# Expert weights fetched as two halves of feature rows, and asked for ahead of the down weights

## The reference

```python
for e in range(N_EXPERTS):            # 32 experts, D_EXPERT = 256
    y = (jax.nn.silu(t @ e_gate[e]) * (t @ e_up[e])) @ e_down[e]
    out = out + combine[:, e:e + 1] * y
```

## Time and profile before

| what | before |
|---|---|
| median of 3 runs | 840.44 us (839.94 to 841.41) |
| the profiled execution | 836.75 us, its span 834.9 us |
| PE busy | 757.1 us (91%) |
| DVE, ACT, POOL busy | 505.1, 428.7, 317.4 us |
| DMA | 160.41 MB, mean 192 GB/s |
| gate, up, down requests | 32 each, 1024.0 KB, median 18.0, 23.0 and 18.7 us to landing |
| chain that ended last | PE 63%, DMA 18%, DVE 7%, ACT 6% of the span |

### The profile page before, as it was taken

The page is one execution under the profiler, slowest core; times in us unless marked ns, Lnnn a source line. Parts: engine busy times, 40 slices in busy tenths (PEclk is TensorE's granted clock), DMA queues, the critical chain, the costliest instruction groups (busy, mean ns, idle before and its releaser), DMA issues.

```text
span 834.9 us, 10616 instructions
## 1 busy us (share of the span) xinstructions
PE 757.1 (91%) x3974; PEld 547.2 (66%) x3974; DVE 505.1 (60%) x774; ACT 428.7 (51%) x636; POOL 317.4 (38%) x240
## 2 busy tenths in 40 slices
PE   3899999999996888899899979999999999989983
PEld 3788888876664555478788856666666666656641
DVE  5641000007766888451347868888888877778827
ACT  6311102116555888630121448878877777677714
POOL 2513354615645776151001134444433333332212
PEclk9999999999999999999999999999999999999998
DMA  8371111100010000241671958999999999999379
GB/s 288 80 201 51 50 29 50 50 1 1 1 47 6 0 1 1 61 141 51 227 258 71 350 163 321 375 382 364 375 376 370 372 373 365 362 363 361 115 265 366
DMA packets 54949, 160.41 MB, mean 192 GB/s; under 512 B 9344, under 2 KB 24160, under 8 KB 46576
## 3 DMA queue, kind: packets, MB, share of 16 engines
q1 hardware_dynamic: 48352, 142.26, 47.3%
q0 software_dynamic: 6400, 16.92, 6.1%
q10 hardware_dynamic: 144, 0.52, 0.2%
HBM read 145.01 MB, written 18.87 MB: 196 GB/s over the span
## 4 chain that ended last, share of the span: by engine, by line
PE 63%; DMA 18%; DVE 7%; ACT 6%; issue 3%; SPq 2%; POOL 0%; DVEq 0%; POOLq 0%; ACTq 0%
DMA wgu<-in_expert_w_up 12%; PE ps L644 6%; PE ps L646 6%; PE ps L645 6%; PE ps L884 5%; PE ps L889 5%; PE ps L892 4%; PE ps L767 3%; PE ps L769 3%; PE ps L768 3%; PE ps L709 3%; PE ps L684 2%; PE ps L911 2%; PE ps L915 2%; PE ps L919 2%
## 5 line engine op out<-in xcount | busy, mean ns | idle before, releaser
L1632 DVE TENSOR_TENSOR wgulo<-wgu,unit 128x2048 fp32r<-128x2048 f32 x64 | 146.4, 2289 | 47.1 <-ACT unit L1174 46.8
L1174 ACT CAST unit<-wgu 128x2048 fp32r<-128x2048 f32 x64 | 122.0, 1907 | 49.2 <-DMA wgu<-in_expert_w_up 47.4
L1880 POOL DMA_INDIRECT expert_rows<-ysb,idx x32 | 53.9, 1685 | 152.2 <-ACT ysb L1221 143.6
L644 PE MATMUL ps<-hThi,whi 128*128 128x512 f32 x224 | 88.8, 396 | 4.2 <-DVE hTlo L1288 4.2
L1873 POOL DMA_INDIRECT xg<-h_rows,idx x32 | 69.3, 2164 | 57.2 <-PE ps L860 40.4
L646 PE MATMUL ps<-hThi,wlo 128*128 128x512 f32 x224 | 88.2, 394 | 0.0
L645 PE MATMUL ps<-hTlo,whi 128*128 128x512 f32 x224 | 88.1, 393 | 0.0
L884 PE MATMUL ps<-unit,xThi 128*80 128x512 f32 x256 | 72.4, 405 | 0.8 <-ACT xThi L1198 0.8
L1638 DVE TENSOR_TENSOR wdlo<-wd,unit 128x2048 fp32r<-128x2048 f32 x32 | 73.1, 2284 | 0.0
L889 PE MATMUL ps<-unit,xTlo 128*80 128x512 f32 x256 | 70.2, 396 | 0.0
L892 PE MATMUL ps<-wgulo,xThi 128*80 128x512 f32 x256 | 69.1, 391 | 0.0
(11 more groups left out here) (203 smaller groups left out, 1498.8 us busy)
## 6 DMA issues: line engine op xcount, KB each, us to landing
wgu<-in_expert_w_gate SPq DMA_DIRECT2D x32, 1024.0 KB, 18.0
wgu<-in_expert_w_up SPq DMA_DIRECT2D x32, 1024.0 KB, 23.0
wd<-in_expert_w_down SPq DMA_DIRECT2D x32, 1024.0 KB, 18.7
y<-expert_rows SPq DMA_DIRECT2D x16, 512.0 KB, 11.1
wraw<-in_w_in SPq DMA_DIRECT2D x14, 512.0 KB, 4.1
xin<-in_x SPq DMA_DIRECT2D x8, 512.0 KB, 5.5
xres<-in_x SPq DMA_DIRECT2D x16, 256.0 KB, 2.9
out<-fo SPq DMA_DIRECT2D x8, 512.0 KB, 7.6
```

Of the source, the lines that this page charges most:

```text
L644: nc.tensor.matmul(bank, whi[i % 2][:, k, :], hThi[:, k, cols], start=(k == 0), stop=False)
L1174: nc.scalar.copy(weight_unit(e, a)[:], raw_half(wgu, e, a)).then_inc(ahi_done, 1)
L1632: nc.vector.tensor_tensor(raw_half(wgulo, e, a), raw_half(wgu, e, a), weight_unit(e, a)[:].bitcast(F32), ALU.subtract).then_inc(alo_done, 1)
```

## The change

Gate and up of an expert are asked for in halves that match TensorE's halves: four requests of 512 KB (4 KB in one piece of each partition) in place of two of 1 MiB, each half behind its own `half_done` count, with a landing semaphore for each half, for which ScalarE waits before each half's cast. In the loop from expert 4 on, the two halves of expert e go ahead of the down weights of e-1. The down weights of expert 3 wait until the first two gathers have landed.

```diff
-        wgu_in = [sem(f"wgu_in{i}") for i in range(RING)]
+        wgu_in = [[sem(f"wgu_in{i}_{a}") for a in range(2)] for i in range(RING)]
...
-            def fetch_expert(e):
+            def fetch_half(e, h):
+                u = e % RING
+                a, b, c = load_expert(e, u, False)
+                ks = slice(4 * h, 4 * h + 4)
+                if e >= RING:
+                    sp.wait_ge(half_done, 2 * (e - RING) + 1 + h)
+                sp.dma_start(wgu[u][:, 0, ks], a[:, ks]).then_inc(wgu_in[u][h], 16)
+                sp.dma_start(wgu[u][:, 1, ks], b[:, ks]).then_inc(wgu_in[u][h], 16)
+
+            def fetch_down(e):
                 u = e % RING
                 a, b, c = load_expert(e, u, False)
                 if e >= RING:
-                    sp.wait_ge(half_done, 2 * (e - RING) + 2)
-                sp.dma_start(wgu[u][:, 0], a).then_inc(wgu_in[u], 16)
-                sp.dma_start(wgu[u][:, 1], b).then_inc(wgu_in[u], 16)
-                if e >= RING:
                     sp.wait_ge(down_done, e - RING + 1)
                 sp.dma_start(wd[u][:], c).then_inc(wd_in[u], 16)
+
+            def fetch_expert(e):
+                fetch_half(e, 0)
+                fetch_half(e, 1)
+                fetch_down(e)
...
             sp.wait_ge(out_mm, 2 * TT)
-            for e in range(2, N_EXP):
-                fetch_expert(e)
+            fetch_expert(2)
+            fetch_half(3, 0)
+            fetch_half(3, 1)
+            sp.wait_ge(xg_in[0], 16)
+            sp.wait_ge(xg_in[1], 16)
+            fetch_down(3)
+            for e in range(RING, N_EXP):
+                fetch_half(e, 0)
+                fetch_half(e, 1)
+                if e > RING:
+                    fetch_down(e - 1)
+            fetch_down(N_EXP - 1)
...
             def half_high(e, a):
 
                 u = 3 * e + a
-                if a == 0:
-                    act.wait_ge(wgu_in[e % RING], 32 * (e // RING + 1))
+                act.wait_ge(wgu_in[e % RING][a], 32 * (e // RING + 1))
```

More of the change, by code:

```diff
@@ L264, in encoder @@
         sq_done = sem("sq_done")
-        eps_added = sem("eps_added")
+        small_done = sem("small_done")
         rstd_a = sem("rstd_a")
@@ L356, in encoder @@
         y_put = [sem(f"y_put{i}") for i in range(2)]
-        v_hots = sem("v_hots")
         v_list_mm = sem("v_list_mm")
@@ L592, in _ @@
             with sp.If(n_ovf > 0):
-                sp.wait_ge(v_lists, 1)
+                sp.wait_ge(v_lists, 2)
                 with sp.Fori(0, N_OVF) as j:
@@ L954, in _ @@
             with pe.If(n_ovf > 0):
-                pe.wait_ge(v_hots, 1)
+                pe.wait_ge(v_lists, 1)
                 for c in range(2 * TT):
@@ L1221, in rows_out @@
                 nc.scalar.copy(ysb[e % 2][:].rearrange("q (n d) -> q n d", n=2), ps[0:CAP, b0:b0 + 2, :]).then_inc(y_out, 1)
-            nc.scalar.activation(junk[:], stat[:, 3, :], ACT.Silu).then_inc(junk_done, 1)
+            nc.scalar.activation(junk[:], stat[:, 3, :], ACT.Silu)
             half_high(0, 1)
@@ L1532, in experts_of @@
                                      misc[:, 12:12 + N_EXP].unsqueeze(1).to_broadcast([P, 2 * TG, N_EXP]), ALU.mult))
-                v.tensor_reduce(ek[:, 2 * TG * g:2 * TG * (g + 1)], mine, AX_X, ALU.add).then_inc(ek_done, 1)
+                v.tensor_reduce(ek[:, 2 * TG * g:2 * TG * (g + 1)], mine, AX_X, ALU.add)
             nc.vector.memset(hx[:], 0.0).then_inc(hx_zero, 1)
@@ L1624, in overflow_lists @@
                 steps_apart(*[v.tensor_tensor(ovf_tile[:, :, a, :], ovf_eq[:], wide(dvals[:, a, :], N_OVF), ALU.mult) for a in range(2)])
-                v.tensor_tensor(ovf_row[:], rows80.to_broadcast([P, 2 * TT, CAP]), wide(row, CAP), ALU.is_equal).then_inc(v_hots, 1)
+                v.tensor_tensor(ovf_row[:], rows80.to_broadcast([P, 2 * TT, CAP]), wide(row, CAP), ALU.is_equal).then_inc(v_lists, 1)
                 dve.wait_ge(v_list_mm, 1)
@@ L1752, in split_low @@
                 gp.tensor_tensor(wlo[i % 2][:], wraw[i % 2][:], whi[i % 2][:].bitcast(F32), ALU.subtract).then_inc(w_split, 1)
[L1754 to L1757, removed]
+            gp.memset(neg_half[:], -0.5).then_inc(small_done, 1)
+            gp.memset(eps_col[:], EPS).then_inc(small_done, 1)
+            pool.wait_ge(small_done, 2)
+            count = [2]
             def inverse_root(src, ready, n, done, t):
                 pool.wait_ge(ready, n)
-                gp.tensor_scalar(stat[:, src + 1, t:t + 1], stat[:, src, t:t + 1], EPS, None, ALU.add).then_inc(eps_added, 1)
+                gp.tensor_scalar(stat[:, src + 1, t:t + 1], stat[:, src, t:t + 1], EPS, None, ALU.add).then_inc(small_done, 1)
                 count[0] += 1
-                pool.wait_ge(eps_added, count[0])
+                pool.wait_ge(small_done, count[0])
                 gp.tensor_tensor(stat[:, src + 1, t:t + 1], stat[:, src + 1, t:t + 1], neg_half[:], ALU.pow).then_inc(done, 1)
@@ L1896, in _ @@
             with pool.If(n_ovf > 0):
-                pool.wait_ge(v_lists, 1)
+                pool.wait_ge(v_lists, 2)
                 with pool.Fori(0, N_OVF) as j:
```

3 lines of the change are left out of this document (removed).

## The result

The changed kernel takes **832.79 us** (median of 9 runs, 827.72 to 835.76), the kernel before 840.44 in the same comparison (9 runs, 836.1 to 841.41). The ratio is 0.9926, interval 0.9904 to 0.9949. It is faster by about 6.2 us by the ratio (7.7 between the two medians), 0.45 of the 13.8 forecast; the range 820.4 to 835.5 holds it. The profiled execution takes 835.62 us (span 833.8, mean granted clock 0.982), of before 836.75 (834.9, 0.986). A second comparison with an unchanged copy gave 830.08 against 837.66, ratio 0.9912 (0.9874 to 0.995).

What follows compares the result with a forecast made beforehand. TensorE was taken to set the pace for the first dozen experts, the weight transfers from about 620 us. Terms 4.5 + 5.5 + 3.8 = 13.8 us, off the 840.44 us median, gave 826.6 us; range 820.4 to 835.5.

Steps and rivals of the forecast that it cites:

- the next wait: Late expert stage: a few us of waiting would appear at the down weights' cast or VectorE's subtraction behind it.
- Costs: SP's queue: two more requests per expert, some 2 us of a 9 us period, hidden because SP mostly waits; taken as 0.
- Part 3: Start of expert stage: expert 3's down weights leave the DMA engines to the first gather; 3.8 us, bounds 0 and 4.5.
- It shifts TensorE's releases, so the whole stream: First gathers: the 3.8 us saved there would move the whole later weight stream earlier.
- The clock's share of it (1.4): Expert 0's first two groups: a shorter TensorE pause avoids the lower clock, gaining 1.4 us, bounds 0 to 1.4.
- The unit itself costs nothing: Expert 3's down weights, asked for later, run where the DMA share is 0.20; without that gap, 2.5 us.
- Part 1: Start of weight stream: requests released at each half put the stream ahead by 4.5 us, bounds 2 and 5.
- Part 2: Transfer-bound later experts: half 0 comes ahead of half 1 and the previous expert's down weights; 5.5 us, bounds 3.3 to 6.7.
- one unit of 3.35 us for each: Mixed weight stream: half 0 stands two one-MiB units earlier, 3.35 us each, 6.7 us together.
- Rival 2: Less than the sum: first gather stays put, the new order gives one unit only; 832.6 us, 834.2 with packets; chance 0.17.
- Rival 3: Full weight stream: each of 54 more requests has its own cost, at 0.5 us giving 853.6 us; chance 0.06.

Runs made afterwards that it cites:

- before_xres_first: Kernel before the change, with the next two residual-row loads issued ahead of expert 0's weights; 833.97 us, ratio 0.9944 to before.
- split_only: Kernel before the change, with every gate and up asked for as two 512 KB requests, same place and release; 843.88 us, ratio 1.0041 to before.
- first_whole: Changed kernel with gate and up of experts 0 and 1 asked for in whole requests; 829.35 us, ratio 0.9883 to before.
- no_gather_wait: Changed kernel with expert 3's down weights asked for at once, not behind the first gathers; 834.68 us, ratio 0.9949 to before.
- order_only: Changed kernel with gate and up whole for all experts, its new order and gather wait kept; 832.09 us, ratio 0.9903 to before.
- halves_old_order: Changed kernel with halves kept, but from expert 4 on down weights of e ahead of the halves of e+1; 832.93 us, ratio 0.9942 to before.
- late_before: Changed kernel, but from expert 12 on whole gate/up requests and down of e ahead of gate/up of e+1; 837.11 us, ratio 0.9971 to before.
- hybrid: Changed kernel with residual rows first and whole gate/up requests for experts 0 to 3 and 8 to 23; 824.11 us, ratio 0.9834 to before.
- after_again: Unchanged copy of the changed kernel; 830.08 us, ratio 0.9912 to before.
- after_third: Second unchanged copy of the changed kernel, its third profiled execution; 829.83 us in one run.

## Why the forecast was right in direction and wrong in size

**Right.** What bounds the kernel, and that the transfers take over from about expert 20. The stall of the transfers begins with expert 22 in the changed kernel (a step of 9.99 us between first products, those before at TensorE's pace) and one or two experts later in its copies, and the next wait is where I put it. Expert 2 to 31 take 272.1, 270.1 and 269.8 us against a forecast of 269. The rate never fell below 367 GB/s. T is 320.4 in the mean of before, its copy and `before_xres_first` (320.9, 318.8, 321.6), and 310.0 in the three executions of the changed one. The expert stage gained 10.4 us of the 13.8.

**The step that failed: "Costs. SP issues five transfers an expert in place of three ... hidden, SP waits most of the time", with the cost of requests taken as 0.** In the steady stretch it holds (`split_only`). At expert 0 SP doesn't wait: small loads on which TensorE depends stand behind the requests. `split_only`, which has the requests and nothing else of the change, is slower by 0.0041, 3.4 us (1.8 to 5.2); `first_whole`, which takes them back for experts 0 and 1 alone, gains 2.4 to 3.6 us by the ratios. In the profiles compared it is 3.2 us, of them 1.6 in every execution and the rest, the clock's, in those where it would not have fallen anyway. I had read SP's queue from 461 us on and not around the first fetch.

**Part 3, down weights of 3 behind the first gathers (forecast 3.8).** The second step that failed is "It shifts TensorE's releases, so the whole stream". By `no_gather_wait` the part is worth 3.1 to 3.8 us at expert 2, as forecast, but 1.6 to 2.2 at expert 31 (2.5 by T). That a saving ahead of a stretch that the transfers bind counts only as far as the transfers start earlier by it fits this, and isn't tested. The clock's share of it (1.4) is no fixed gain: behind the first transposes the clock fell in one of the changed kernel's three executions and stayed in the old kernel's copy. The 0.91 that the prediction sets against 1.99 us for the first group comes from the chain; the timeline has 1.13 for such a group at full clock. The term of 1.4 was taken from starts and doesn't depend on it. "The unit itself costs nothing" is in line with the runs.

**Part 1, requests at each half (forecast 4.5).** The mechanism holds. The idle at the start fell from 13.8 to 4.4 us (mean of three), 9.4, where parts 1 and 3 together had forecast 8.3. What of this reaches the end is not settled: `order_only` has 8.0 us of idle and the same T (310.8). `halves_old_order` shows 6 us of T for halves with part 3 and without the order.

**Part 2, what comes first (forecast 5.5, bounds 3.3 to 6.7).** The term adds up two things, that the down weights go behind and that half 0 no longer waits for half 1. Taken back together from expert 12 on (`late_before`) they are worth 6.7 us by T, 4.3 with the idle taken off, 3.8 to 5.0 by the medians: within the bounds. What is wrong is the way to it, one unit of 3.35 us for each. The order alone, taken back beside halves, is worth 2.0 by T; order alone gives T = 310.8 and 312.4, halves alone from expert 12 on 312.0, both 310.0, neither 316.7. Either one gives nearly all.

**The sum by what was measured:** the 13.8 less 3.4 in T (of which part 3 is 1.6 to 2.2, and the other 1.2 to 1.8 lie within the scatter of T and can't be given to a part) and less 3.4 for the requests is 7.0; the medians show 6.2 (by the ratio) and 7.4 (second comparison). **Rival 2**, less than the sum, was the nearest, 832.6, but by luck: of its conditions, the gather that stays where it is didn't come, part 2 gave more than its one unit, and the 3.4 us of the requests are not in it. **Rival 3**, a cost per request in the full stream, is refuted. The Trainium skill (DMA: Bandwidth & Descriptors, Rules for kernel authors) asks for 1 MiB or more per transfer for the most bandwidth; in the full queue of this kernel requests of 512 KB run at 374 GB/s in `split_only`, those of 1 MiB at 371 in before, so the measurement shows no loss there.

**Open.** Why halves and order are not additive, and how much of the removed idle comes through to the end. From expert 25 to 26 every kernel has a step of 10.9 to 13.1 us (12.22 before, 11.91 after) that I can't explain.

## What to carry to other kernels

Before splitting requests, look at every place where the queue is issued and not only at the steady loop: 1.3 us more of issue ahead of a small load that TensorE waits for cost 1.6 to 3.4 us of a gain of 10.4, and putting that load first gave 9 us over the changed kernel (823.84, ratio to before 0.9796 against 0.9926). In a stage bound by transfers, test two remedies for the same wait both alone and together: here either of order and halves gave nearly all of what both gave, and adding up their gains one by one would count it twice. When such a wait goes, look for the next thing that is late. A microsecond saved ahead of such a stretch need not arrive at its end: of 3.1 to 3.8 us at expert 2, 1.6 to 2.2 were left at expert 31.

## What the runs showed of the hardware

- SP's own instruction gets longer when much is queued: 0.33 to 0.48 us per request at the first fetch, but in the full stretch single ones take up to 6 us, and one of `hybrid` took 8.90 (the old kernel stays under 2.3, `late_before` under 1.7). In the changed kernel and in `order_only`, respectively:

```profile
690.85 5.47 SPq L560 DMA_DIRECT2D wgu<-in_expert_w_gate  x1
```

```profile
713.22 5.66 SPq L573 DMA_DIRECT2D wgu<-in_expert_w_up  x1
```

  The DMA share is 1.02 and 0.98 meanwhile (0.96 in `hybrid`), so the transfers don't run dry.
- Behind TensorE's pause at the residual rows, the granted clock stayed at 1.00 after 3.18 us in the old kernel, and fell to 0.50 after 3.39 in its copy; it fell with every pause of 4.6 to 4.9 us, in eight executions. One group of transposes then takes 1.97 us (1.67 in `after_again`) in place of 1.09.
- Ahead of the first gathered rows the length of the pause doesn't tell whether the clock falls. It fell to 0.60 behind 0.73 us in `hybrid` and to 0.58 behind 1.92 in `after_third`, and stayed at 1.00 behind 2.13 in `after_again`. Expert 1's first product then comes 10.7 us after the first transposes in place of 9.15.
- Pieces of 4 KB and of 8 KB move at the same rate in the mixed stream (374 and 371 GB/s).
